# Mixture-of-experts products on TensorE: matmuls of one width issued together, half a weight tile at a time

## The chip, the cores and the metric

One core of a Trainium2 chip runs the whole step as a single launch. The metric is the device time of that launch in microseconds (us), the median of repeated runs on one chip. The kernel is written engine by engine: TensorE (PE), VectorE (DVE), ScalarE (ACT), GpSimd (POOL) and SyncE (SP) each have their own instruction stream, and they wait for each other on semaphores that the program names. All data are fp32.

## What is computed

The program is one inference step of a two-layer backbone over 384 tokens (128 context, 256 latent) of width 1024. Each layer has a mixer (gated linear attention with windowed attention in layer 0, RWKV-7 in layer 1) and then a mixture of experts. Only the mixture of experts bears on this change:

```python
def hier_moe(h, w_grp, b_grp, w_exp, b_exp, w_gate, w_up, w_down):
    ...
    gates = jnp.sum(jax.nn.one_hot(idx, N_EXPERTS, dtype=f32) * wts[..., None], axis=1)
    hid = jax.nn.silu(jnp.einsum('td,edf->tef', t, w_gate)) * jnp.einsum('td,edf->tef', t, w_up)
    hid = hid * gates[..., None].astype(hid.dtype)
    return jnp.einsum('tef,efd->td', hid, w_down).reshape(B, L, D)
```

There are 16 experts (4 groups of 4) a layer; a token goes to two experts of one group. An expert has gate and up matrices of 1024 x 512 each and a down matrix of 512 x 1024.

## The kernel before, in words

**Weights.** All large weights stream from HBM as tiles of 128 partitions x 2048 words (1 MB) through a ring of six slots in SBUF (`ring`). SP (`stream`, L256) issues one DMA a tile, and waits for `w_used` before it overwrites a slot; PE increments `w_used` with the last matmul that reads a tile, and waits in `tile_in` (L277) until a tile has landed. An expert takes exactly six tiles: four of gate/up weights (L1390, `gate_up(e, h, half)`: `h` is the half of the hidden width, `half` the half of the contraction over D = 1024) and two of down weights (L1412, `down(e, f)`, two values of `f` a tile).

**Tokens.** The router sorts (token, expert) pairs by expert; an expert gets at most CAP = 96 rows. If no expert has more, the branch with `gathered_pe`, `gathered_act` and `gathered_dve` runs, as here. `TOKE` holds the expert's 96 tokens, transposed (128 partitions x 8 chunks x 96). In every product the tokens are the stationary operand and the weights move. The 96 tokens are split into MANY = 64 and FEW = 32: the 64 are a stationary block of 64 columns of the array, and two such matmuls (`x` = 0, 1) stand side by side in the two column halves; the 32 are a block of 32 columns, and four such matmuls (`x` = 0 to 3) stand side by side in the four column quarters. So one contraction step `kk` of gate/up is two matmuls of 64 columns x 256 moving columns (L1398) and four of 32 columns x 128 moving columns (L1401), and one step `f` of down is two of 64 x 512 (L1418) and four of 32 x 256 (L1423). The profile records an fp32 matmul as two instructions (two passes over the moving columns), each with its own weight load (PEld).

**One expert on PE** (L1428, `expert`) is, in this order: gate_up(0,0), gate_up(0,1), gate_up(1,0), turn_hidden(0), gate_up(1,1), down 0, turn_hidden(1), down 1, down 2, down 3. In a tile the steps go one after another, and each step issues its 64-wide and then its 32-wide matmuls. `turn_hidden(h)` (L1405) turns the gated hidden rows of half `h` (ACT's silu L1493/L1494, then DVE's product L1577, which signals `s_hid`) with four transposes: a block of 64 rows and one of 32 rows for each of two chunks, in turns. DVE copies the result to `HIDG` (L1580, `s_tts`), the stationary operand of down.

**Around it.** ACT loads the next expert's tokens (L1488), and ACT (L1501) and DVE (L1592) copy an expert's products to `ROWE`, from where ACT's queue sends 96 rows to HBM (L1509). Expert 0 stands ahead of the loop: it takes its tokens straight from a selection matmul, while POOL scatters all token rows to HBM in sorted order (L1618) and reads them back in six blocks (L1622). PE turns these after expert 0 (`turn_sorted`, L1371, L1387), ACT and DVE store them (`TOK`), and expert 1 begins. Experts 1 to 13 are a loop (`pe.Fori`), 14 and 15 stand behind it. In expert 15 three blocks of mixed token rows, gathered back by POOL (L1627) and mixed by DVE (L1559, L1560), are turned between the down products (`turn_mixed`, L1363), and DVE adds them to the state (L1568); then eight banks of last products follow (L1467, L1468).

Of the kernel before, what the change touches and what calls it, by code (L numbers as in the profile page):

```python
# [26 lines left out]
P = 128  # L27
D = 1024
KC = D // P
# [6 lines left out]
HD = 64  # L36
# [7 lines left out]
CAP = 96  # L44
MANY, FEW = 64, 32
# [158 lines left out]
def build(nc, xT, cst, rcst, vec, sinkr, ckT, cv, zgla, zrwkv, wrt, brt, dec2, wa2, wstream,  # L204
# [6 lines left out]
    def sem(name):  # L211
        return ctx.enter_context(nc.semaphore(name))
# [4 lines left out]
    with ctx:  # L217
# [19 lines left out]
        def bank(b, cols=T, at=0):  # L237
            return ps[:, b * 512 + at:b * 512 + at + cols]

        def area(at, words, **dims):  # L240
            v = A[:, at:at + words]
            if not dims:
                return v
            names = " ".join(dims)
            return v.rearrange(f"p ({names}) -> p {names}", **dims)

        w_in = [sem(f"weight_tile_in_slot{i}") for i in range(RING)]
        w_used = sem("weight_tiles_used")
# [28 lines left out]
        def tile_in(pe, n, i=0):  # L277

            pe.wait_ge(w_in[n % RING], i * 16 + 16 * (n // RING + 1))

        def tile(n, **dims):
            names = " ".join(dims)
            return ring[:, n % RING * TILE:(n % RING + 1) * TILE].rearrange(f"p ({names}) -> p {names}", **dims)
# [806 lines left out]
        def moe_block(l, at, end, squares):  # L1090
# [49 lines left out]
            HIDG = area(o4, 4 * CAP, f=4, s=CAP)  # L1140
# [14 lines left out]
            TOKE = area(o7 + 2 * GU, KC * CAP, k=KC, s=CAP)  # L1155
# [194 lines left out]
            with nc.Block() as block:  # L1350
# [8 lines left out]
                def mixed(a, k):  # L1359
                    return bank((2, 6, 2)[a] + k // 4, P, P * (k % 4))  # L1360

                def gathered_pe(pe):
                    def turn_mixed(a):  # L1363
                        pe.wait_ge(s_y, a + 1)
                        if a == 2:
                            pe.wait_ge(s_t0a, 1)
                        for k in range(KC):
                            mm = pe.transpose(mixed(a, k), YR[:, 0, a, P * k:P * k + P], ident)
                        mm.then_inc(s_t0, 1)

                    def turn_sorted():  # L1371
                        pe.wait_ge(s_sell, 1)
                        for y in range(2):
                            for a in range(3):
                                mm = pe.transpose(bank(6 + y, P, P * a)[0:CAP], SELL[:, y, a, :], ident)
                        mm.then_inc(s_turn_l, 1)
                        for g in range(12):
                            b, half = divmod(g, 2)
                            if half == 0:
                                pe.wait_ge(s_rin[b], 16)  # L1380
                            if g == 2:
                                pe.wait_ge(s_gh, 1)
                            if g >= 4:
                                pe.wait_ge((s_hg, s_hd)[half], b - 1)
                            for x in range(4):
                                k = 4 * half + x
                                mm = pe.transpose(bank(TURN_BANKS[g % 4], P, P * x), RB[:, b, P * k:P * k + P], ident)  # L1387
                            mm.then_inc(s_ga, 1)

                    def gate_up(e, h, half):  # L1390
                        tile_in(pe, at + 2 * h + half, e)
                        w = tile(at + 2 * h + half, k=4, w=2, c=256)
                        for kk in range(4):
                            k = 4 * half + kk
                            if (h, half, kk) == (1, 0, 3):
                                pe.wait_ge(s_hid, e * 2 + 1)
                            for x in range(2):
                                pe.matmul(bank(h, 256)[HD * x:HD * x + HD], TOKE[:, k, 0:MANY], w[:, kk, x, :],  # L1398
                                          start=k == 0, stop=k == KC - 1)
                            for x in range(4):  # L1400
                                mm = pe.matmul(bank(2 + h, P)[FEW * x:FEW * x + FEW], TOKE[:, k, MANY:CAP],  # L1401
                                               w[:, kk, x // 2, x % 2 * P:x % 2 * P + P], start=k == 0, stop=k == KC - 1)
                        mm.then_inc(w_used, 1)

                    def turn_hidden(h):  # L1405
                        for c in range(2):
                            pe.transpose(bank(6 + c, MANY), HIDR[HD:P, h, P * c:P * c + P], ident[HD:P, HD:P])
                            r = slice(HD + FEW * c, HD + FEW * c + FEW)
                            mm = pe.transpose(bank(6 + c, FEW, MANY), HIDR[r, h, 256:GU], ident[r, r])  # L1409
                        mm.then_inc(s_tt, 1)  # L1410

                    def down(e, f):  # L1412
                        w = tile(at + 4 + f // 2, f=2, c=D)
                        if f % 2 == 0:
                            pe.wait_ge(s_tts, e * 2 + (f // 2 + 1))
                            tile_in(pe, at + 4 + f // 2, e)
                        for x in range(2):
                            pe.matmul(bank(4, 512)[HD * x:HD * x + HD], HIDG[:, f, 0:MANY], w[:, f % 2, 512 * x:512 * x + 512],  # L1418
                                      start=f == 0, stop=f == 3)
                        if f == 0:  # L1420
                            pe.wait_ge(s_hid, e * 2 + 2)
                        for x in range(4):
                            mm = pe.matmul(bank(5, 256)[FEW * x:FEW * x + FEW], HIDG[:, f, MANY:CAP],  # L1423
                                           w[:, f % 2, 256 * x:256 * x + 256], start=f == 0, stop=f == 3)
                        if f % 2:
                            mm.then_inc(w_used, 1)

                    def expert(e, last=False):  # L1428
                        first = isinstance(e, int) and e == 0
                        if not first:  # L1430
                            pe.wait_ge(s_tok, e)
                        gate_up(e, 0, 0)
                        gate_up(e, 0, 1)
                        gate_up(e, 1, 0)
                        turn_hidden(0)
                        gate_up(e, 1, 1)
                        if not first:
                            pe.wait_ge(s_ous, e)
                            pe.wait_ge(s_ousa, e)
                        down(e, 0)  # L1440
                        turn_hidden(1)
                        down(e, 1)
                        if last:
                            turn_mixed(0)
                        down(e, 2)
                        down(e, 3)
                        if last:
                            turn_mixed(1)
                            turn_mixed(2)

                    pe.wait_ge(s_tf, 2)
                    pe.wait_ge(s_sl, 1)
                    expert(0)
                    turn_sorted()
                    with pe.Fori(1, NE - KEPT) as e:
                        expert(e)
                    expert(NE - 2)
                    expert(NE - 1, last=True)
                    pe.wait_ge(s_gh, 1)
                    pe.wait_ge(s_ous, NE)  # L1460
                    pe.wait_ge(s_ousa, NE)
                    for n, b in enumerate(FINAL_BANKS):
                        if b == 6:
                            pe.wait_ge(s_t0a, 2)
                        if b == 2:
                            pe.wait_ge(s_t0a, 3)
                        pe.matmul(bank(b), ROWE[0:CAP, 0, P * n:P * n + P], GH[0:CAP, 0, :], start=True, stop=False)  # L1467
                        pe.matmul(bank(b), ROWE[0:CAP, 1, P * n:P * n + P], GH[0:CAP, 1, :], start=False,  # L1468
                                  stop=True).then_inc(s_fin, 1)
# [1192 lines left out]
```

## Time and profile before

| | before |
|---|---|
| median of 3 runs | 1827.23 us (1827.18 to 1830.56) |
| the profiled execution's own time | 1828.28 us |
| its span, first to last instruction | 1826.4 us |
| mean granted TensorE clock | 0.957 of full |
| PE busy | 1645.4 us, 90% of the span |
| DVE, ACT, POOL busy | 613.3, 526.5, 265.1 us (34%, 29%, 15%) |
| moved by DMA | 328.33 MB, mean 180 GB/s |

The two mixtures of experts lie at about 383 to 770 us and 1414 to 1800 us of the span. A PE that is shown busy is not a PE at its peak, since the ends of pipelined matmuls are modelled; how long work takes is therefore read here from the starts of neighbouring rows, not from busy sums.

### The profile page before, as it was taken

The numbers are of one execution on the slowest core, as the hardware profiler recorded it, in microseconds if no ns is written. First come the engines' busy times: TensorE is split into PE (matmuls) and PEld (weight loads), VectorE is DVE, ScalarE is ACT, GpSimd is POOL, SyncE is SP. The second block draws the span as 40 slices with busy tenths as digits, with TensorE's granted clock in tenths as the row PEclk, the third lists the DMA queues.
The fourth block names the chain that finished last, engine by engine and source line by source line (L and its number), as shares of the span: only waits on it lengthen the run. The fifth ranks groups of instructions, "written<-read, shape, count | busy, mean of one in ns | idle before, by whom it ended". The sixth has DMA issues, their size and how long they took to land. (4 is left out here: it accounts for less than half of the span.)

```text
span 1826.4 us, 41121 instructions
## 1 busy us (share of the span) xinstructions
PE 1645.4 (90%) x17678; PEld 888.8 (49%) x17678; DVE 613.3 (34%) x1520; ACT 526.5 (29%) x1202; POOL 265.1 (15%) x260
## 2 busy tenths in 40 slices
PE   3997968889999999959998889989877999999997
PEld 1554554453333333435557777777744433333333
DVE  2004762341111111450306766666615111111115
ACT  3114543221111111120135666565413111111112
POOL 0000040020000000010044555555001000000010
PEclk9998998999999999979999999898989999999999
DMA  9225549376878887812200000000033787788891
GB/s 390 98 98 193 226 191 374 119 286 227 287 282 288 289 292 283 313 46 92 104 12 5 6 6 5 5 6 4 6 140 134 282 287 287 285 286 288 286 342 41
DMA packets 54036, 328.33 MB, mean 180 GB/s; under 512 B 6646, under 2 KB 10038, under 8 KB 18712
## 3 DMA queue, kind: packets, MB, share of 16 engines
q1 hardware_dynamic: 43632, 290.07, 43.2%
q0 software_dynamic: 5184, 18.88, 2.6%
q10 hardware_dynamic: 5096, 17.58, 2.5%
q8 instruction: 96, 1.57, 0.4%
q14 instruction: 28, 0.23, 0.0%
HBM read 304.35 MB, written 22.16 MB: 179 GB/s over the span
## 5 line engine op out<-in xcount | busy, mean ns | idle before, releaser
L1398 PE MATMUL ps<-ring,arena 128*64 128x256 f32 x2048 | 336.2, 407 | 6.3 <-ACT arena L1488 5.2
L1401 PE MATMUL ps<-ring,arena 128*32 128x128 f32 x4096 | 219.2, 286 | 0.0
L298 PE MATMUL ps<-HT,ring 128*128 128x384 f32 x544 | 180.6, 496 | 14.2 <-PEq L367 8.2
L1401 PEld LDWEIGHTS ps<-ring,arena 128*32 128x32 f32 x4096 | 81.0, 108 | 198.5 <-issue 198.5
L1577 DVE TENSOR_TENSOR arena<-arena,ps 64x256 f32<-64x256 f32 (+1 forms) x128 | 40.6, 357 | 344.7 <-ACT arena L1494 344.7
L1398 PEld LDWEIGHTS ps<-ring,arena 128*64 128x64 f32 x2048 | 101.9, 135 | 109.7 <-issue 106.9
L1493 ACT ACTIVATE arena<-ps 64x256 f32<-64x256 f32 x64 | 24.1, 377 | 443.1 <-PE ps L1401 443.1
L298 PEld LDWEIGHTS ps<-HT,ring 128*128 128x128 f32 x544 | 105.4, 194 | 89.2 <-issue 19.7
L1418 PE MATMUL ps<-ring,arena 128*64 128x512 f32 x512 | 138.1, 618 | 0.0
L1627 POOL DMA_INDIRECT arena<-moe_rows,arena x12 | 11.4, 952 | 674.1 <-DMA moe_rows<-arena 671.1
L1501 ACT ACTIVATE arena<-ps 32x256 f32<-32x256 f32 x128 | 48.0, 375 | 198.0 <-PE ps L1423 196.9
L298 PE MATMUL ps<-arena,ring 128*128 128x384 f32 x256 | 85.4, 498 | 18.8 <-DVEq L2026 18.8
L1423 PE MATMUL ps<-ring,arena 128*32 128x256 f32 x1024 | 81.8, 391 | 10.1 <-DVE arena L1577 10.1
L1592 DVE COPY arena<-ps 64x512 f32<-64x512 f32 x64 | 44.0, 688 | 135.4 <-PE ps L1423 134.7
L322 PE MATMUL ps<-ring,arena 128*32 128x256 f32 x768 | 55.3, 442 | 23.8 <-DMA ring<-wstream 14.6
L1423 PEld LDWEIGHTS ps<-ring,arena 128*32 128x32 f32 x1024 | 20.1, 108 | 116.2 <-issue 77.9
L298 PEld LDWEIGHTS ps<-arena,ring 128*128 128x128 f32 x256 | 49.8, 195 | 54.5 <-DVEq L2026 19.5
L1580 DVE COPY arena<-ps 128x192 f32<-128x192 f32 x64 | 22.9, 358 | 152.2 <-PE ps L1409 152.2
L2431 PE MATMUL ps<-ring 64*64 64x32 f32 x1536 | 59.3, 228 | 13.0 <-DVE ring L2288 8.3
L2431 PEld LDWEIGHTS ps<-ring 64*64 64x64 f32 x1536 | 53.0, 143 | 36.3 <-DVE ring L2288 17.6
L2431 PE MATMUL ps<-ring,arena 64*64 64x32 f32 x1536 | 61.7, 232 | 2.3 <-DVE arena L2313 2.3
L2431 PEld LDWEIGHTS ps<-ring,arena 64*64 64x64 f32 x1536 | 55.4, 149 | 7.3 <-issue 4.3
(357 smaller groups left out, 2300.6 us busy)
## 6 DMA issues: line engine op xcount, KB each, us to landing
ring<-wstream SPq DMA_DIRECT2D x272, 1024.0 KB, 5.2
moe_rows<-arena ACTq DMA_DIRECT2D x28, 384.0 KB, 4.7
arena<-moe_tokens POOLq DMA_DIRECT2D x12, 512.0 KB, 10.6
moe_rows<-arena ACTq DMA_DIRECT2D x4, 512.0 KB
consts<-cst ACTq DMA_DIRECT2D x1, 1655.0 KB, 17.1
XT<-xT ACTq DMA_DIRECT2D x1, 1536.0 KB, 11.1
yT<-HT SPq DMA_DIRECT2D x3, 384.0 KB, 3.2
arena<-wa SPq DMA_DIRECT2D x1, 1024.0 KB, 4.8
```

The source lines that it names most:

```text
L298: mm = pe.matmul(bank(m % 8), w[:, k, m % 2 * P:m % 2 * P + P], rhs[:, k, :], start=k == 0, stop=k == KC - 1)
L322: mm = pe.matmul(bank(b, 256)[32 * g:32 * g + 32], SC[:, k, :], w[:, a, g, :], start=k == 0, stop=k == KC - 1)
L1398: pe.matmul(bank(h, 256)[HD * x:HD * x + HD], TOKE[:, k, 0:MANY], w[:, kk, x, :], start=k == 0, stop=k == KC - 1)
L1401: mm = pe.matmul(bank(2 + h, P)[FEW * x:FEW * x + FEW], TOKE[:, k, MANY:CAP], w[:, kk, x // 2, x % 2 * P:x % 2 * P + P], start=k == 0, sto ...
L1418: pe.matmul(bank(4, 512)[HD * x:HD * x + HD], HIDG[:, f, 0:MANY], w[:, f % 2, 512 * x:512 * x + 512], start=f == 0, stop=f == 3)
L1423: mm = pe.matmul(bank(5, 256)[FEW * x:FEW * x + FEW], HIDG[:, f, MANY:CAP], w[:, f % 2, 256 * x:256 * x + 256], start=f == 0, stop=f == 3)
L1493: act.activation(HIDR[HD:P, h, 0:256], bank(h, 256)[0:HD], ACT.Silu)
L1501: last = act.activation(ROWE[MANY:CAP, kept, 256 * x:256 * x + 256], bank(5, 256)[FEW * x:FEW * x + FEW], ACT.Copy)
L1577: hid = dve.tensor_tensor(x, x, bank(b, GU - 256 if b > 1 else 256)[HD:P], ALU.mult)
L1580: dve.tensor_copy(HIDG[:, 2 * h:2 * h + 2, :], ps[:, 3072:4096].rearrange("p (f s) -> p f s", f=2)[:, :, 0:CAP]).then_inc(s_tts, 1)
L1592: copy = dve.tensor_copy(ROWE[0:MANY, kept, 512 * x:512 * x + 512], bank(4, 512)[HD * x:HD * x + HD])
L2431: mm = pe.matmul(bank(o, 32, 32 * n)[h], dn(left)[h, d, n], right[h, d, n], start=True, stop=True)
```

## The change

In `gate_up` the four steps of a tile are split by width: `many()` issues the 64-wide matmuls of all four steps, `few()` the 32-wide ones. A tile with `half` = 0 issues `many()` then `few()`, one with `half` = 1 the reverse, so that at a border between two tiles the same width goes on. `turn_hidden` issues its two transposes of 64 rows first and its two of 32 rows then. `down(e, f)` becomes `down_many` and `down_few`, called from `expert` in an order that goes on with the same width from one step to the next. The wait for the second half's hidden product (`s_hid`, e * 2 + 2) moves from between the 64-wide and the 32-wide matmuls of step 0 to behind both. The number and the shapes of matmuls are the same, and so is the code of the other engines.

```diff
+                        def many():
+                            for kk in range(4):
+                                k = 4 * half + kk
+                                for x in range(2):
+                                    mm = pe.matmul(bank(h, 256)[HD * x:HD * x + HD], TOKE[:, k, 0:MANY], w[:, kk, x, :],
+                                                   start=k == 0, stop=k == KC - 1)
+                            return mm
...
+                        if half:
+                            few()
+                            mm = many()
+                        else:
+                            many()
+                            mm = few()
                         mm.then_inc(w_used, 1)
...
                         for c in range(2):
                             pe.transpose(bank(6 + c, MANY), HIDR[HD:P, h, P * c:P * c + P], ident[HD:P, HD:P])
+                        for c in range(2):
                             r = slice(HD + FEW * c, HD + FEW * c + FEW)
                             mm = pe.transpose(bank(6 + c, FEW, MANY), HIDR[r, h, 256:GU], ident[r, r])
                         mm.then_inc(s_tt, 1)
...
-                        down(e, 0)
+                        pe.wait_ge(s_tts, e * 2 + 1)
+                        w = down_tile(e, 0)
+                        down_many(w, 0)
+                        down_few(w, 0)
+                        pe.wait_ge(s_hid, e * 2 + 2)
+                        down_few(w, 1)
                         turn_hidden(1)
-                        down(e, 1)
+                        down_many(w, 1).then_inc(w_used, 1)
                         if last:
                             turn_mixed(0)
-                        down(e, 2)
-                        down(e, 3)
+                        w = down_tile(e, 1)
+                        pe.wait_ge(s_tts, e * 2 + 2)
+                        down_many(w, 2)
+                        down_few(w, 2)
+                        down_few(w, 3)
+                        down_many(w, 3).then_inc(w_used, 1)
```

PE in the loop over experts, before: the last steps of gate_up(1,0), the first turn of hidden rows and the first step of gate_up(1,1). A row is a line of the kernel, what is written and read (`ps` is PSUM, `ring` the weights, `arena` the tokens or hidden rows), the shape of the product and a count of matmuls.

```order
L1398 MATMUL ps<-ring,arena 64x256 x2
L1401 MATMUL ps<-ring,arena 32x128 x4
L1396 ISA
L1398 MATMUL ps<-ring,arena 64x256 x2
L1401 MATMUL ps<-ring,arena 32x128 x4
L1407 MATMUL ps<-consts,arena 128x64
L1409 MATMUL ps<-consts,arena 128x32
L1407 MATMUL ps<-consts,arena 128x64
L1409 MATMUL ps<-consts,arena 128x32
L1398 MATMUL ps<-ring,arena 64x256 x2
L1401 MATMUL ps<-ring,arena 32x128 x4
```

The same place now, from gate_up(0,0) to the end of gate_up(1,1):

```order
L1398 MATMUL ps<-ring,arena 64x256 x8
L1408 MATMUL ps<-ring,arena 32x128 x32
L1398 MATMUL ps<-ring,arena 64x256 x16
L1408 MATMUL ps<-ring,arena 32x128 x12
L1406 ISA
L1408 MATMUL ps<-ring,arena 32x128 x4
L1422 MATMUL ps<-consts,arena 128x64 x2
L1425 MATMUL ps<-consts,arena 128x32 x2
L1408 MATMUL ps<-ring,arena 32x128 x16
L1398 MATMUL ps<-ring,arena 64x256 x8
```

Sixteen pairs of a 64-wide and a 32-wide row became five rows of one width each and a part of a sixth, and the wait of the first turn (ISA) still stands ahead of the last step's 32-wide matmuls of gate_up(1,0).

PE in the same loop, before: down steps 0 and 1 with the second turn between them (steps 2 and 3 repeat the last two rows).

```order
L1418 MATMUL ps<-ring,arena 64x512 x2
L1421 REGISTER_ALU
L1423 MATMUL ps<-ring,arena 32x256 x4
L1407 MATMUL ps<-consts,arena 128x64
L1409 MATMUL ps<-consts,arena 128x32
L1407 MATMUL ps<-consts,arena 128x64
L1409 MATMUL ps<-consts,arena 128x32
L1418 MATMUL ps<-ring,arena 64x512 x2
L1423 MATMUL ps<-ring,arena 32x256 x4
```

The same place now, all four down steps:

```order
L1434 MATMUL ps<-ring,arena 64x512 x2
L1440 MATMUL ps<-ring,arena 32x256 x4
L1460 REGISTER_ALU
L1440 MATMUL ps<-ring,arena 32x256 x4
L1422 MATMUL ps<-consts,arena 128x64 x2
L1425 MATMUL ps<-consts,arena 128x32 x2
L1434 MATMUL ps<-ring,arena 64x512 x4
L1440 MATMUL ps<-ring,arena 32x256 x8
L1434 MATMUL ps<-ring,arena 64x512 x2
```

The 32-wide matmuls of step 1 now stand ahead of the turn, the 64-wide ones of steps 1 and 2 follow each other, and the last 64-wide row runs into the next expert's first one. REGISTER_ALU works out the value for the wait on `s_hid`, which stands there.

## Rows read from the trace of the kernel before

**Rows 1.** Windows, layer 0's loop: PE, PEld, DVE, ACT, POOL (x), clock, DMA share, GB/s.

```profile
440.00:500.00 60.00, 59.37 (x666) 21.68 (x664) 9.08 (x21) 8.88 (x24) 0.00 (x0) 1.00 0.83 297
```

**Rows 2.** Waits, 440 to 740 us: who waited for whom, total us, times, longest.

```profile
ACT arena L1493 <- PE ps L1401: 177.1, 26, 7.7
PE ps L1423 <- DVE arena L1577: 4.1, 13, 0.3
```

**Rows 3.** PE timeline, one expert: start, us, line, out<-in, stationary, moving, count.

```profile
560.68 0.65 PE L1398 MATMUL ps<-ring,arena 128*64 128x256 f32 x4
561.26 0.42 PE L1401 MATMUL ps<-ring,arena 128*32 128x128 f32 x8
561.62 0.65 PE L1398 MATMUL ps<-ring,arena 128*64 128x256 f32 x4
...
568.19 0.27 PE L1407 MATMUL ps<-consts,arena 64*128 64x64 f32 x1
...
568.94 0.65 PE L1398 MATMUL ps<-ring,arena 128*64 128x256 f32 x4
...
572.70 1.08 PE L1418 MATMUL ps<-ring,arena 128*64 128x512 f32 x4
574.10 0.64 PE L1423 MATMUL ps<-ring,arena 128*32 128x256 f32 x8 [0.32 <-DVE arena L1577]
...
577.00 1.08 PE L1418 MATMUL ps<-ring,arena 128*64 128x512 f32 x4
578.01 0.64 PE L1423 MATMUL ps<-ring,arena 128*32 128x256 f32 x8
578.58 1.08 PE L1418 MATMUL ps<-ring,arena 128*64 128x512 f32 x4
...
591.42 0.27 PE L1407 MATMUL ps<-consts,arena 64*128 64x64 f32 x1
```

**Rows 4.** PE timeline, stages before the experts: runs of one width.

```profile
281.58 3.66 PE L322 MATMUL ps<-ring,arena 128*32 128x256 f32 x64
291.47 1.07 PE L322 MATMUL ps<-ring,arena 128*32 128x256 f32 x16 [1.41 <-DMA ring<-wstream]
...
212.17 0.87 PE L655 MATMUL ps<-arena 128*64 128x128 f32 x6
```

**Rows 5.** Windows: layer 1's mixer, with many small matmuls (columns as rows 1).

```profile
1311.80:1314.80 3.00, 3.00 (x113) 2.37 (x113) 1.66 (x6) 2.88 (x7) 0.00 (x0) 1.00 0.03 5
```

**Rows 6.** Windows: a stretch in which the weight stream is never idle (columns as rows 1).

```profile
280.00:290.00 10.00, 9.41 (x129) 6.36 (x128) 1.71 (x6) 1.70 (x5) 0.00 (x0) 1.00 1.01 424
```

**Rows 7.** PE timeline, layer 0: start of expert 0, its end, start of expert 1.

```profile
382.58 0.65 PE L1398 MATMUL ps<-ring,arena 128*64 128x256 f32 x4 [0.58 <-ACT arena L1255]
...
405.81 0.86 PE L1375 MATMUL ps<-consts,arena 128*96 128x128 f32 x6
...
416.08 0.65 PE L1398 MATMUL ps<-ring,arena 128*64 128x256 f32 x4 [2.45 <-ACT arena L1488]
...
417.10 1.12 PE L1398 MATMUL ps<-ring,arena 128*64 128x256 f32 x4
418.15 0.66 PE L1401 MATMUL ps<-ring,arena 128*32 128x128 f32 x8
```

**Rows 8.** POOL's reads of the sorted token rows, six a layer (line L1622).

```profile
L1622 POOL DMA_DIRECT2D arena<-moe_tokens x12: 527/550/580, 388.0 to 1422.5; - x12
DMA to landing us min/median/max: 4.0/10.6/18.4
```

**Rows 9.** DVE timeline, expert 15 of layer 0: second turn's copy, product copies.

```profile
761.39 0.36 DVE L1580 COPY arena<-ps 128x192 f32<-128x192 f32 x1 [1.48 <-PE ps L1409]
...
768.06 1.39 DVE L1592 COPY arena<-ps 64x512 f32<-64x512 f32 x2
```

**Rows 10.** PE timeline, same place: start of the eight last products.

```profile
769.55 0.88 PE L1467 MATMUL ps<-arena 96*128 96x384 f32 x2 [0.37 <-issue]
```

**Rows 11.** POOL's gathers of rows to mix, six a layer (line L1627).

```profile
L1627 POOL DMA_INDIRECT arena<-moe_rows,arena x12: 933/937/1007, 727.1 to 1764.5; - x12
DMA to landing us min/median/max: 11.0/15.3/18.9
```

More of the change, by code:

```diff
@@ L1392, in gate_up, with few @@
                         w = tile(at + 2 * h + half, k=4, w=2, c=256)
[L1393 to L1402, printed above, removed]
+                        def many():
[5 more added lines that the diff above has]
+                            return mm
+                        def few():
+                            for kk in range(4):
+                                k = 4 * half + kk
+                                if (h, half, kk) == (1, 0, 3):
+                                    pe.wait_ge(s_hid, e * 2 + 1)
+                                for x in range(4):
+                                    mm = pe.matmul(bank(2 + h, P)[FEW * x:FEW * x + FEW], TOKE[:, k, MANY:CAP],
+                                                   w[:, kk, x // 2, x % 2 * P:x % 2 * P + P], start=k == 0, stop=k == KC - 1)
+                            return mm
+                        if half:
[4 more added lines that the diff above has]
+                            mm = few()
                         mm.then_inc(w_used, 1)
@@ L1410, in turn_hidden, with down_tile, down_many, down_few @@
                         mm.then_inc(s_tt, 1)
[L1412 to L1416, printed above, removed]
+                    def down_tile(e, j):
+                        tile_in(pe, at + 4 + j, e)
+                        return tile(at + 4 + j, f=2, c=D)
+                    def down_many(w, f):
                         for x in range(2):
[L1418 to L1421, printed above, removed]
+                            mm = pe.matmul(bank(4, 512)[HD * x:HD * x + HD], HIDG[:, f, 0:MANY],
+                                           w[:, f % 2, 512 * x:512 * x + 512], start=f == 0, stop=f == 3)
+                        return mm
+                    def down_few(w, f):
                         for x in range(4):
@@ L1424, in down @@
                                            w[:, f % 2, 256 * x:256 * x + 256], start=f == 0, stop=f == 3)
-                        if f % 2:
-                            mm.then_inc(w_used, 1)
+                        return mm
                     def expert(e, last=False):
```

## The prediction

> **What bounds the kernel now.** I read the windows first. In the loop over experts PE is busy 59.37 of 60 us at the full granted clock, VectorE and ScalarE 9 us each, and the DMA engines 0.83 of the time [rows 1]. The waits say the same: ScalarE waits for PE (177 us in 300), PE for others only 4.1 us, 0.3 a time, always in the same place: the product of the second hidden half [rows 2]. So an expert lasts as long as PE takes for it: 591.42 - 568.19 = 23.23 us from one first turn to the next [rows 3].
>
> Is PE at its peak in there? The timeline of one expert gives the steps from start to start [rows 3]: a gate/up step is 0.58 us of 64-wide and 0.36 us of 32-wide matmuls, a down step 1.01 and 0.57 us, a turn 0.75 us, and the first down step 1.40 us for its 64-wide part because of the wait. These add up: 16 x 0.94 + 4 x 1.58 + 2 x 0.75 + 0.39 = 23.2 us.
>
> Then I looked for a place where matmuls of one width follow each other without a change. Before the experts, 32-wide matmuls with 256 moving columns, four side by side, do so with new weights each: 64 instructions (16 passes of four) in 3.66 us, 16 instructions (4 passes) in 1.07 us [rows 4]. Twelve more passes cost 2.59 us, 0.216 us a pass of 256 columns, that is 0.108 for 128 and 0.43 for 512. The 64-wide kind shows the same pace: six in a row with 128 columns last 0.87 us; less the 0.27 that one takes at the end, that is 0.60 us for five steps with a start of some 0.05, 0.11 each [rows 4]. With these paces the steps of [rows 3] split:
>
> - gate/up 64-wide: 0.58 = 2 passes x 0.216 + 0.15; 32-wide: 0.36 = 2 x 0.108 + 0.14.
> - down 64-wide: 1.01 = 2 x 0.43 + 0.15; 32-wide: 0.57 = 2 x 0.216 + 0.14.
>
> So each change of width costs 0.14 to 0.15 us, whatever the columns: the array is filled and emptied without overlap. An expert pays this some 40 times, and that is a quarter of its time.
>
> **What the change does, part by part.**
>
> *Gate/up and down.* The columns stay: 32 passes x 0.216 + 32 x 0.108 + 8 x 0.43 + 8 x 0.216 = 15.5 us an expert. The runs of one width become, around the loop: four 64-wide ones (down 3 with the next expert's gate_up(0,0); gate_up(0,1) with (1,0); gate_up(1,1) with down 0; down 1 with 2) and five 32-wide ones ((0,0) with (0,1); (1,0); (1,1); down 0 with 1; down 2 with 3). That is 4 x 0.15 + 5 x 0.14 = 1.3 us where 20 x 0.29 = 5.8 us were paid.
>
> *Turns.* Four transposes in 0.75 us had a change at each; two of these go. Bounds: 0.38 us, if each pair costs as much as one, and 0.75. I take 0.75 - 2 x 0.14, about 0.5, so 1.0 an expert for 1.5.
>
> *The moved wait.* PE needs the second hidden product 1.40 us after down's first matmul starts [rows 3]. It now has down 0 of both widths ahead of it: 0.86 + 0.15 + 0.43 = 1.44 us. Gate_up(1,1) now ends with its 64-wide matmuls, so ScalarE may start slightly later. I leave 0.1 us for 0.39. Queued behind this wait are down 1 and the turn; DVE, which copies the turn, waits for them, and then down 2 for DVE, with 1 us of 64-wide matmuls (down 1) as cover against a copy of 0.36 us [rows 9].
>
> Sum for an expert: 15.5 + 1.3 + 1.0 + 0.1 = 17.9 us, **5.3 us less**. Bounds from the turns, the wait and the rounding: 17.5 to 18.4.
>
> *Weights.* Six tiles of 1.05 MB and 0.39 MB of rows an expert are 6.68 MB. Where the stream is never idle it moves 424 GB/s [rows 6], so 15.8 us: the stream hides below 17.9 us, but with a tenth to spare instead of a third. It is the next in line.
>
> *Expert 0.* It begins at 382.58 and ends at 405.81 [rows 7]; it will end near 400.5. But expert 1 needs the six blocks of sorted rows, and the last one lands 18.4 us after an issue at about 390.7 (the first issue is at 388.0, each takes about 0.55 us) [rows 8]: at 409.1. From there, 0.9 us of transposes, the last copies and the load of tokens remain, some 3.8 us: expert 1 starts at about 412.9 instead of 416.08 [rows 7]. Gain 3.2 of the 5.3 us; the rest turns into a wait for POOL's reads. They share the engines with a weight stream that comes sooner, so 1 us either way.
>
> *Expert 15.* Behind the second turn, DVE is the bound: from its copy at 761.39 to the end of the products' copies at 769.45 it has no pause to speak of [rows 9], and the last products start right then, at 769.55 [rows 10]. What PE gains behind that turn (3 x 1.58 us become 3.9) is lost: 0.8 us. Gain 4.5 us.
>
> *All.* A layer: 3.2 + 14 x 5.3 + 4.5 = 82 us; two layers 164 us. Against the profiled execution's 1828.3 us (1.1 above the median of the runs, so the same within a thousandth) that is 1664. I add 2 us: the gathers of rows to mix take up to 18.9 us to land [rows 11], and will come nearer to their use in expert 15. Forecast: **1666 us**.
>
> **A rule that speaks against it.** The rows above show weight loads that hide: 0.216 us a pass in the run of 64 is the same 0.84 ns a column as the step from 256 to 512 moving columns within the experts (1.08 - 0.65 = 0.43 us for 512 columns in two passes) [rows 3, 4], so nothing of a load is in it. The Trainium skill, "TensorE: Matmul & The Clock Gate", section "The mechanism" of Part 3, says that a weight load overlaps running matmuls only if its row group differs; here all products use all 128 rows. By that rule every pass would pay its load, and the change would lose most of its gain; the trace does not agree for the 32-wide kind.
>
> **Rivals.**
>
> 1. *The weight stream becomes the bound.* For: 0.83 of the engines' time is taken at 23.23 us an expert [rows 1], which is 19.3 us of busy time, more than 17.9. Against: that includes the waiting of each transfer's first packets, which a denser stream would hide, and in [rows 6] it moves 424 GB/s. If 19.0 us an expert stay, the gain is 14 x 4.2 + 3.2 + 3.4 = 65 us a layer: 1697. Chance 0.15.
> 2. *PE cannot be fed.* In long 32-wide runs of gate/up one matmul must start every 0.108 / 4 = 27 ns. For: the longest run in [rows 4] has only one in 54 ns. If that were the limit, 32 passes would cost 0.108 more, 3.5 us an expert: a gain of 1.8 us, about 1771 at worst; halfway, 1717. Against: 113 instructions in 3.00 us, one in 26.5 ns, in the mixer [rows 5]. Chance 0.07.
> 3. *Loads are paid in every pass.* The first pass in a run is longer than the next by some 0.05 us (64-wide) and 0.03 us (32-wide) for its load; paid 40 times each, that is 3.2 us an expert, a gain of 2.1 us: some 1760. That is the page's rule as a mechanism of this kernel. Chance 0.03.
> 4. *The change does only half of what it says:* the pause stands between steps of 64-wide matmuls too (the trace shows their runs only with 128 columns on one column half [rows 4]). 20 x 0.15 = 3.0 instead of 0.6 us, a gain of 2.9 us: 1738. Chance 0.04.
> 5. *Slower:* PE loses its full clock. In expert 1, after PE has stood idle 2.45 us, a 64-wide step takes 418.15 - 417.10 = 1.05 us instead of 0.58, as at half the clock [rows 7]. If PE now stops for each tile, the same could go on through the loop; an expert at half clock would take about 15.5 x 2 + 2.4 = 33.4 us, 15.5 more than at full. It would outweigh the gain of 5.3 us from a third of the experts on, and give some 2110 us in all. Against: 1.00 in the loop now, with waits of 0.3 us in it [rows 1, 2]. Chance 0.02.
>
> **How the numbers follow.** The forecast has 0.68 and lies between 1652 (turns at 0.38 us, restart 1 us sooner, rounding) and 1682 (18.4 us an expert). Rival 1 adds 1682 to 1706, and with it the low end of rival 2: 0.84 in all. So the range is 1652 to 1706. Remaining chances lie above it. About 0.2% can be told from no change: faster by more 0.97, the same 0.01, slower 0.02.
>
> **What would show it.** In the profile after: experts 17.9 us apart by the first turn; 64-wide runs of gate/up of 16 passes at 0.216, 32-wide ones at 0.108 us; the wait in front of down 1's 32-wide matmuls at or below 0.2 us; DMA share near 0.95 and no PE wait for `ring`; expert 1 near 413 us, released by the row blocks. PE waits for weight tiles, or passes longer than these, would show where I am wrong.

## The result, and the profile after

The changed kernel takes 1682.41 us (median of 4 runs, 1680.07 to 1689.40), the kernel before beside it 1827.20: a ratio of 0.921, interval 0.918 to 0.924. Five more runs (experiment 10) give 1684.39 us and the same ratio. The forecast was 1666, the range 1652 to 1706. So the direction and most of the size came as worked out, and 16 us are missing. The profiled execution takes 1680.41 us with a span of 1678.6; that is 147.8 less than the span before, and this difference is what the rows below split up.

The head of the page after: span, then busy time, share of the span and instructions of each engine.

```profile
span 1678.6 us, 41121 instructions
PE 1494.4 (89%) x17678; PEld 957.6 (57%) x17678; DVE 613.7 (37%) x1520; ACT 526.4 (31%) x1202; POOL 265.2 (16%) x260
```

PE does the same products in 151 us less busy time, and DVE and ACT are busy as long as before. The same stretch of the loop as [rows 1], in the windows of the changed kernel (us, PE, PEld, DVE, ACT, POOL with counts, clock, DMA share, GB/s):

```profile
440.00:500.00 60.00, 60.00 (x854) 34.96 (x852) 11.80 (x28) 12.31 (x33) 0.00 (x0) 1.00 0.97 369
```

The clock stays at 1.00, PE gets through 854 instructions in place of 666, and the DMA share goes from 0.83 to 0.97. Read alone, that share says that the weight stream is all but the bound. The waits of the changed kernel from 420 to 660 us (who for whom, total, times, longest), which answer to [rows 2], say otherwise:

```profile
ACT arena L1518 <- PE ps L1398: 129.7, 27, 7.5
PEld ps L1440 <- DVE arena L1602: 4.7, 13, 0.4
```

These are two lines of the list; no wait of PE for `ring` stands in it. ACT still waits for PE, and the wait for the second hidden product is now one of the weight load alone (0.4 us at most). The PE timeline of one expert after, which answers to [rows 3] (start, us, line, out<-in, stationary, moving, count):

```profile
573.00 0.34 PE L1422 MATMUL ps<-consts,arena 64*128 64x64 f32 x2
573.26 0.25 PE L1425 MATMUL ps<-consts,arena 32*128 32x32 f32 x2
573.44 1.08 PE L1408 MATMUL ps<-ring,arena 128*32 128x128 f32 x32
574.45 1.95 PE L1398 MATMUL ps<-ring,arena 128*64 128x256 f32 x16
576.23 1.03 PE L1434 MATMUL ps<-ring,arena 128*64 128x512 f32 x4
577.19 1.16 PE L1440 MATMUL ps<-ring,arena 128*32 128x256 f32 x16
578.28 0.33 PE L1422 MATMUL ps<-consts,arena 64*128 64x64 f32 x2
...
584.32 1.96 PE L1408 MATMUL ps<-ring,arena 128*32 128x128 f32 x64
586.21 3.67 PE L1398 MATMUL ps<-ring,arena 128*64 128x256 f32 x32
589.81 1.08 PE L1408 MATMUL ps<-ring,arena 128*32 128x128 f32 x32
590.82 0.33 PE L1422 MATMUL ps<-consts,arena 64*128 64x64 f32 x2
```

From first turn to first turn it is now 590.82 - 573.00 = **17.82 us**, where 17.9 was forecast and 23.23 was before. Sixty-four 32-wide instructions (16 passes) last 586.21 - 584.32 = 1.89 us: 16 x 0.108 = 1.73 and one change of 0.16. Thirty-two 64-wide ones (16 passes) last 3.60 us: 16 x 0.216 = 3.46 and one change of 0.14. A turn is 0.44 us, where about 0.5 was taken.

So the loop gives what was promised. The missing microseconds lie at its two ends. This is the PE timeline between expert 0 and expert 1 of layer 0 after, which answers to [rows 7]; a bracket holds the idle time ahead and what ended it:

```profile
384.47 1.95 PE L1398 MATMUL ps<-ring,arena 128*64 128x256 f32 x16 [0.58 <-ACT arena L1255]
...
402.44 0.86 PE L1375 MATMUL ps<-consts,arena 128*96 128x128 f32 x6
...
407.71 1.82 PE L1387 MATMUL ps<-consts,arena 128*128 128x128 f32 x8 [0.97 <-DMA arena<-moe_tokens]
412.38 5.58 PE L1387 MATMUL ps<-consts,arena 128*128 128x128 f32 x24 [2.84 <-DMA arena<-moe_tokens]
420.41 2.59 PE L1398 MATMUL ps<-ring,arena 128*64 128x256 f32 x16 [2.45 <-ACT arena L1513]
```

Expert 0 ends 18.0 us after its start (23.2 before), but expert 1 starts 35.9 us after that same start, where it was 33.5 before. PE waits for the sorted row blocks. Two windows of that stretch, one during the waits and one behind them (columns as above):

```profile
408.00:412.00 4.00, 1.53 (x8) 1.13 (x6) 0.69 (x1) 0.60 (x1) 0.00 (x0) 0.50 1.02 422
412.40:418.00 5.60, 5.56 (x24) 4.68 (x24) 1.38 (x2) 1.80 (x3) 0.00 (x0) 0.50 0.33 134
```

While PE waits, the DMA engines move 422 GB/s, about as much as in [rows 6]; of the 1.69 MB in this window, 0.88 MB are weights that nobody needs yet, and 0.44 MB belong to the blocks. Then the ring is full and the engines rest. In and after its waits PE is granted 0.50 of its clock (1.2 GHz), and it has not the whole clock back when expert 1 begins: 16 64-wide instructions take 2.59 us here and 1.95 in expert 0. POOL's reads of these blocks after, to be held against [rows 8]:

```profile
L1647 POOL DMA_DIRECT2D arena<-moe_tokens x12: 527/551/580, 392.2 to 1352.4; - x12
DMA to landing us min/median/max: 5.9/15.2/21.2
```

The median landing went from 10.6 to 15.2 us. The last block of layer 0 now lands at 415.95 us, 31.5 us after expert 0 began, where it was 26.5 us. The six reads are issued within 2.7 us and land one after another: in layer 0 before, the last four at 398.19, 401.96, 405.30 and 409.06 us, and now at 407.67, 412.33, 414.21 and 415.95. At the other end, expert 15 of layer 0 (PE timeline after, the place of [rows 9, 10]):

```profile
695.94 1.94 PE L1368 MATMUL ps<-consts,arena 128*128 128x128 f32 x8 [4.15 <-DVEq L1596]
697.68 1.48 PE L1492 MATMUL ps<-arena 96*128 96x384 f32 x2
```

PE stands idle for 4.15 us before the last mixed block, and the last products begin at a granted clock of 0.50 (1.48 us for a pair that took 0.88 before [rows 10]). DVE's mixing (DVE timeline) waits for the gathers just ahead of it:

```profile
691.60 0.75 DVE L1584 TENSOR_SCALAR arena<-arena 128x1024 f32<-128x1024 f32 x1 [3.37 <-DMA arena<-moe_rows,arena]
```

POOL's gathers after, which answer to [rows 11]:

```profile
L1652 POOL DMA_INDIRECT arena<-moe_rows,arena x12: 933/937/1007, 663.4 to 1629.7; - x12
DMA to landing us min/median/max: 8.1/13.6/21.9
```

By stage, before against after, taken from the two timelines (layer 0, layer 1; "first turn" is DVE's copy behind it). The forecast's terms are divided at the first turns here: of expert 1's 5.3 us of gain, 2.9 lie ahead of its first turn, so that 3.2 becomes 6.1 for the first stage and 4.5 becomes 1.6 for the last.

| stage | forecast, a layer | measured, layer 0 | measured, layer 1 |
|---|---|---|---|
| start of expert 0 to expert 1's first turn | -6.1 | -0.6 | -0.5 |
| the next 14 first turns | -74.2 | -75.7 | -75.7 |
| expert 15's first turn to the end of its last products (layer 1: to their start) | -1.6, and +2 for both layers together | +4.4 | -1.2 |

That sums to -149.3 us; the other stages, which the change doesn't touch, gave 1.5 back (1.9 of them ahead of the first expert).

### The profile page after: what moved, and what is told of

It reads as the page before. It is cut to its first block and busy times, and to the rows that moved or that the text cites. A ratio compares the mean times of both kernels' runs of the same rounds, so it can differ in the third digit from the quotient of the medians.

```text
span 1678.6 us, 41121 instructions
## 1 busy us (share of the span) xinstructions
PE 1494.4 (89%) x17678; PEld 957.6 (57%) x17678; DVE 613.7 (37%) x1520; ACT 526.4 (31%) x1202; POOL 265.2 (16%) x260
## 5 line engine op out<-in xcount | busy, mean ns | idle before, releaser
L1398 PE MATMUL ps<-ring,arena 128*64 128x256 f32 x2048 | 243.2, 385 | 6.3 <-ACT arena L1513 5.2
L1398 PEld LDWEIGHTS ps<-ring,arena 128*64 128x64 f32 x2048 | 141.9, 137 | 97.0 <-issue 36.0
L1408 PE MATMUL ps<-ring,arena 128*32 128x128 f32 x4096 | 133.8, 278 | 0.0
L1434 PE MATMUL ps<-ring,arena 128*64 128x512 f32 x512 | 129.8, 605 | 0.0
L1408 PEld LDWEIGHTS ps<-ring,arena 128*32 128x32 f32 x4096 | 107.7, 111 | 27.0 <-issue 25.4
L322 PE MATMUL ps<-ring,arena 128*32 128x256 f32 x768 | 55.9, 445 | 25.1 <-DMA ring<-wstream 15.8
L1440 PE MATMUL ps<-ring,arena 128*32 128x256 f32 x1024 | 71.2, 388 | 0.0
L1440 PEld LDWEIGHTS ps<-ring,arena 128*32 128x32 f32 x1024 | 23.4, 108 | 68.9 <-issue 51.9
## 6 DMA issues: line engine op xcount, KB each, us to landing
arena<-moe_tokens POOLq DMA_DIRECT2D x12, 512.0 KB, 15.2
```

What stands on the lines that cost most here:

```text
L322: mm = pe.matmul(bank(b, 256)[32 * g:32 * g + 32], SC[:, k, :], w[:, a, g, :], start=k == 0, stop=k == KC - 1)
L1398: mm = pe.matmul(bank(h, 256)[HD * x:HD * x + HD], TOKE[:, k, 0:MANY], w[:, kk, x, :], start=k == 0, stop=k == KC - 1)
L1434: mm = pe.matmul(bank(4, 512)[HD * x:HD * x + HD], HIDG[:, f, 0:MANY], w[:, f % 2, 512 * x:512 * x + 512], start=f == 0, stop=f == 3)
```

## The experiments

Experiments 1 to 4 and 8 are one execution each, and their readings rest on the timelines more than on the times.

**1. The turns alone.** The kernel before, with the transposes of 64 rows ahead of those of 32:

```diff
                         for c in range(2):
                             pe.transpose(... 64 rows ...)
+                        for c in range(2):
                             pe.transpose(... 32 rows ...)
```

> Before, with the transposes of hidden rows issued by height alone. Theory (each change of shape on the array costs about 0.145 us): two of the five changes of a turn go, and the changed kernel's trace shows 0.44 us for a turn instead of 0.75, so an expert takes 23.23 - 0.62 = 22.6 us and the kernel about 1827 - 28 x 0.62 = 1809 us. Rival (the gain of the turns is hidden behind the wait for the second hidden product): 0.31 us an expert or less, 22.9 us, 1818 us.

Measured: 1810.98 us beside 1826.73. The PE timeline of the loop:

```profile
540.86 0.33 PE L1407 MATMUL ps<-consts,arena 64*128 64x64 f32 x2
541.12 0.25 PE L1410 MATMUL ps<-consts,arena 32*128 32x32 f32 x2
541.30 0.65 PE L1398 MATMUL ps<-ring,arena 128*64 128x256 f32 x4
...
563.47 0.33 PE L1407 MATMUL ps<-consts,arena 64*128 64x64 f32 x2
```

A turn is 0.44 us for 0.75, and an expert 22.61 for 23.23: 0.31 a turn for two changes fewer, 0.155 each. A change of the height of transposes costs what a change of width does.

**2. Gate/up alone.** The kernel before with the new `gate_up` (`many()`, `few()`, the reverse in every second tile), and turns and down as before. The diff is that part of the change.

> Before, with only gate/up grouped by width (tiles with half 1 in reverse); turns and down as before. Theory (a constant price a change of width): 27 of the changes go, 27 x 0.145 = 3.9 us, against which the wait for the second hidden product grows by some 0.1 us since the last 64-wide matmuls now stand right before down: 19.4 us an expert, kernel about 1725 us. Rival (the price belongs to other things, such as a new bank or a new accumulation step): an expert stays within 1 us of 23.2.

Measured: 1731.27 us beside 1826.73, so this part gives most of the gain. The PE timeline of the loop:

```profile
543.05 0.27 PE L1422 MATMUL ps<-consts,arena 64*128 64x64 f32 x1
...
556.00 1.95 PE L1408 MATMUL ps<-ring,arena 128*32 128x128 f32 x64
557.88 3.67 PE L1398 MATMUL ps<-ring,arena 128*64 128x256 f32 x32
...
562.50 0.27 PE L1422 MATMUL ps<-consts,arena 64*128 64x64 f32 x1
```

An expert takes 19.45 us, 3.78 less than before, for 27 changes fewer with 0.13 us of longer wait for the hidden product set against them: 0.145 a change. Sixty-four instructions in 1.88 us are one per 29 ns, so PE is fed (rival 2), and a pass doesn't pay its load (rival 3).

**3. Without the reversal.** The changed kernel, each gate/up tile as `many()` and then `few()`:

```diff
-                        if half:
-                            few()
-                            mm = many()
-                        else:
-                            many()
-                            mm = few()
+                        many()
+                        mm = few()
```

> The changed kernel without the reversal: every gate/up tile issues its 64-wide, then its 32-wide matmuls. Theory: twelve runs of one width an expert instead of nine, 3 x 0.145 = 0.43 us more: 18.2 to 18.3 us an expert, and the kernel some 28 x 0.43 = 12 us slower than the changed one, about 1693 us. Rival (the weight stream, busy 0.98 of the time, is what sets 17.82 us): no change at 17.8 us.

Measured: 1686.66 us. The PE timeline has 573.52 - 555.35 = 18.17 us from first turn to first turn:

```profile
555.35 0.33 PE L1418 MATMUL ps<-consts,arena 64*128 64x64 f32 x2
...
559.69 1.07 PE L1436 MATMUL ps<-ring,arena 128*32 128x256 f32 x16
560.69 0.33 PE L1418 MATMUL ps<-consts,arena 64*128 64x64 f32 x2
...
573.52 0.33 PE L1418 MATMUL ps<-consts,arena 64*128 64x64 f32 x2
```

The expert is longer by 0.35 us as soon as PE has more changes to pay. That is less than the 0.43 of three changes, because the wait at down 0 went: its 16 32-wide instructions take 560.69 - 559.69 = 1.00 us here and 1.09 in the changed kernel. With that, three changes cost 0.44 us. Had the weight stream set the 17.82 us, these would have been hidden: PE sets them.

**4. One width, the old order.** The kernel before, whose four 32-wide products of a gate/up step are replaced by two 64-wide ones with 128 moving columns:

```diff
-                            for x in range(4):
-                                mm = pe.matmul(bank(2 + h, P)[FEW * x:FEW * x + FEW], TOKE[:, k, MANY:CAP],
-                                               w[:, kk, x // 2, x % 2 * P:x % 2 * P + P], start=k == 0, stop=k == KC - 1)
+                            for x in range(2):
+                                mm = pe.matmul(bank(2 + h, P)[HD * x:HD * x + HD], TOKE[:, k, FEW:CAP],
+                                               w[:, kk, x, 0:P], start=k == 0, stop=k == KC - 1)
```

> Before, in its old order, with the 32-wide gate/up products replaced by 64-wide ones of 128 moving columns, two side by side (they take other tokens and leave half of the weights' columns out; the passes and columns in time stay the same). Theory (the width change is what costs): no pause is left in a gate/up step, 2 x 0.216 + 2 x 0.108 = 0.65 us instead of 0.94; 31 changes go, so 23.23 - 4.5 = 18.7 us an expert, though nothing is grouped. Rival (the pause comes with a change of bank, of moving length or of accumulation step, whatever the width): 0.94 us a step and 23.2 us an expert stay.

Measured: 1707.65 us; an expert takes 559.80 - 540.91 = 18.89 us. Two steps in the PE timeline:

```profile
540.91 0.27 PE L1407 MATMUL ps<-consts,arena 64*128 64x64 f32 x1
...
542.36 0.60 PE L1398 MATMUL ps<-ring,arena 128*64 128x256 f32 x4
542.79 0.39 PE L1401 MATMUL ps<-ring,arena 128*64 128x128 f32 x4
543.01 0.60 PE L1398 MATMUL ps<-ring,arena 128*64 128x256 f32 x4
...
559.80 0.27 PE L1407 MATMUL ps<-consts,arena 64*128 64x64 f32 x1
```

A step is 543.01 - 542.36 = 0.65 us, three passes of 0.216 and no pause at all, though the two products still alternate between different moving sizes, banks and weights. So what costs 0.14 to 0.15 us is the change of the stationary block's width itself, neither the order nor the new accumulator. A step also has two products fewer here, but four side by side cost no pause by themselves: experiment 2 has sixteen such passes in a row without one. The Trainium skill, "TensorEngine Tiling (Array Packing)", "Key Properties", says that a change of the tiling mode, as against a change of the tile, drains TensorE. The trace agrees as far as a pause at each such change shows, with 0.58 + 0.36 us a step before [rows 3] and 0.65 here.

**5. The weight stream held for the row blocks.** The changed kernel; SP waits in each layer for the sixth block (in the branch without sorted blocks POOL signals the same semaphore itself) before it issues the tiles of expert 1:

```diff
                     route_sp(sp)
+                    sp.wait_ge(s_rin[5], 16)
                     stream(sp, end)
...
                 def general_pool(pool):
+                    pool.sem_inc(s_rin[5], 16)
```

> The changed kernel, with SP holding the refills of the weight ring in each mixture until the sixth block of sorted rows has landed. Theory (the gap between expert 0 and expert 1 is long because the refills, asked for sooner, share the DMA engines with the scatter and the six blocks): the sixth block lands near 16 us after the start of expert 0 instead of 31, expert 1 then starts about 10.3 us after the end of expert 0 as it did before (ScalarE and VectorE storing the blocks bound it), 7 us sooner in each layer: about 1667 us. Rival (the blocks are slow by themselves): expert 1 starts where it did, 36 us after expert 0. Second rival (the held tiles come too late): experts 1 and 2 wait for the ring, and the gain is lost, about 1680 us.

Measured: **1662.23 us** (1661.36 to 1663.01), a ratio of 0.9086 to before, interval 0.9069 to 0.9104, beside 0.921 for the changed kernel. The reads of the blocks, and PE between expert 0 and 1:

```profile
L1648 POOL DMA_DIRECT2D arena<-moe_tokens x12: 527/554/580, 391.7 to 1343.1; - x12
DMA to landing us min/median/max: 3.6/7.5/9.5
```

```profile
384.62 1.95 PE L1399 MATMUL ps<-ring,arena 128*64 128x256 f32 x16 [0.58 <-ACT arena L1255]
...
405.83 4.56 PE L1388 MATMUL ps<-consts,arena 128*128 128x128 f32 x40 [1.50 <-ACT arena L1504]
412.83 1.95 PE L1399 MATMUL ps<-ring,arena 128*64 128x256 f32 x16 [2.45 <-ACT arena L1514]
```

The slowest block lands after 9.5 us instead of 21.2, PE no longer waits for any, and in layer 0 expert 1 starts 28.2 us after expert 0 instead of 35.9. Its first 16 instructions take 1.95 us, so the stretch at half the clock is gone too. Up to expert 1's first turn that makes 9.4 us in each layer, 7.7 and 6.6 of them by the earlier start. The stream catches up: no wait for `ring` follows in the loop, which stays at 17.82 us an expert.

**6. The prefetch held for the gathers.** The changed kernel; SP issues the mixture's own tiles, and waits for the last gathered rows before it prefetches for the stage behind:

```diff
                     route_sp(sp)
+                    stream(sp, at + N_MOE)
+                    sp.wait_ge(s_yin[2], 32 * l + 32)
                     stream(sp, end)
```

> The changed kernel, with SP holding the six tiles of the next block until POOL's gathers of rows to mix have landed. Theory (layer 0's last turn of mixed rows waits 4.15 us because the gathers share the engines with the prefetch, while layer 1, which has none, does not wait): the last gather lands some 16 us after its issue instead of 21.9, the wait goes, and the last products keep the full clock (0.88 us a pair instead of 1.48): 4 to 6 us less, about 1675 us. Rival (the gathers are slowed by the last experts' own tiles): the wait stays, within 1 us of 1680.

Measured: 1682.95 us (1676.45 to 1685.20), no less than the changed kernel. In its place the edit works. The PE timeline of expert 15's end in layer 0, and what follows it:

```profile
691.79 1.06 PE L1370 MATMUL ps<-consts,arena 128*128 128x128 f32 x8 [0.69 <-DVEq L1598]
693.22 0.88 PE L1494 MATMUL ps<-arena 96*128 96x384 f32 x2 [0.37 <-issue]
...
704.72 5.44 PE L1757 MATMUL ps<-arena,consts 128*128 128x384 f32 x16 [0.91 <-ACT arena L1764]
```

The idle time ahead of the last block falls from 4.15 to 0.69 us, and the products start at full speed; the slowest gather lands after 15.3 us instead of 21.9, and the idle 3.37 us of DVE ahead of the mixing are gone. From the first turn's copy (679.78 here, 680.49 in the changed kernel) to the next stage (704.72 and 709.90) it is 24.9 us instead of 29.4: 4.5 us, of which the next stage takes up to 0.9 as a wait of its own. The profiled executions differ by 4 us, the medians don't. The medians leave the worth of this edit open.

**7 and 9. Both holds.** Both edits together, twice, on two chips.

> Both holds together. Theory: the two gains lie in different places and add, 14 + 5 us: about 1662 us. Rival (what is saved at the head returns as waits for weights in the loop): not below 1670 us.

> Both holds once more, with more runs and beside the changed kernel on the same chip. Theory (14 to 18 us from the hold at the head, 5 from the one at the tail, both shown by the traces): 20 us below the changed kernel, 1655 to 1665 us, where the spread comes from the granted clock in layer 1's mixer, which no version touches. Rival (the tail's hold is worth nothing, as the median of that hold alone would have it): the same as the hold for the blocks alone, 1662 us.

Measured: 1658.96 us (1655.49 to 1664.68), then 1663.91 (1656.68 to 1666.56): ratios 0.906 and 0.909 to the kernel before, intervals 0.9035 to 0.9086 and 0.9065 to 0.9112. Against the hold for the blocks alone (0.9086) no difference is shown by the times. The stage itself is shorter: from the copy behind expert 15's first turn to the end of the last products, layer 0 takes 24.0 us in both profiled executions and 29.2 in experiment 5. A likely reason for the scatter stands in a stage that none of these edits touches, the mixer of layer 1. Windows from 870 to 1260 us (columns as above), experiment 5, then the second run of both holds:

```profile
870.00:1260.00 390.00, 340.96 (x6786) 280.12 (x6784) 250.62 (x591) 221.39 (x497) 183.66 (x159) 0.93 0.02 5
```

```profile
870.00:1260.00 390.00, 342.14 (x6722) 282.38 (x6720) 250.28 (x586) 215.57 (x487) 180.88 (x158) 0.90 0.02 5
```

The granted clock is 0.93 and 0.90, and from the first to the last of the stage's most frequent products (L2458 and L2460) it is 351.5 and 359.9 us. The difference of 8.4 us is more than the edit at the tail is worth; experiment 6 has a clock of 0.94 here, experiment 7 one of 0.90. The mean clock of whole executions points the same way: with both holds, the three that took 1655.5 to 1656.7 us had 0.952 to 0.955, the six that took 1662.1 to 1666.6 us had 0.943 to 0.949. Why the clock of this stage differs stays open.

**8. Half the steps.** The changed kernel, with two of the four contraction steps in each gate/up tile, so that PE has less to do for the same stream:

```diff
-                            for kk in range(4):
+                            for kk in (2, 3):
...
```

The same stands in both `many()` and `few()`, and the first of the two steps left starts the sum.

> The changed kernel with half of the gate/up steps left out (each tile's first two), so that PE needs 17.82 - 16 x 0.216 - 16 x 0.108 = 12.6 us an expert while the weights to load stay the same. It measures where the weight stream becomes the bound. Theory (the stream at its pace of 424 GB/s): 6.68 MB take 15.8 us, an expert lasts 15.8 to 16.5 us and PE waits for the ring. Rival (a busy share of 0.98 at 376 GB/s means that the stream is already at its limit in the changed kernel): 17.5 to 17.8 us an expert.

Measured: 1614.92 us. An expert takes 15.8 us; the windows, and the waits from 440 to 600 us:

```profile
440.00:500.00 60.00, 50.54 (x600) 23.48 (x596) 12.81 (x30) 12.60 (x34) 0.00 (x0) 1.00 1.01 424
```

```profile
PEld ps L1434 <- DMA ring<-wstream: 20.9, 11, 2.2
PE ps L1434 <- DMA ring<-wstream: 16.0, 10, 1.7
```

This is what a loop bound by the stream looks like: PE 50.5 of 60 us, waits for `ring`, 424 GB/s at a share of 1.01. The floor of 15.8 us is the forecast's 6.68 MB at the rate of [rows 6], and 2 us below the changed kernel's expert. A share of 0.97 at 369 GB/s was not that bound.

**10. The changed kernel again**, beside experiment 9 on the same chip, unedited.

> The changed kernel, unaltered, for comparison on the same chip as the version with both holds: 1680 to 1690 us, as measured before.

Measured: 1684.39 us (1679.09 to 1690.48), ratio 0.921, interval 0.9185 to 0.9235. Experiment 9 beside it, with both holds, is 20 us faster.

## Why the prediction was right, and where it was off

**The price of a change of width: right.** 0.14 to 0.15 us was forecast; experiments 1 to 4 measure 0.14 to 0.155, and 4 shows that the width is the cause.

**Long runs at 0.216 and 0.108 us a pass: right**, up to 16 passes. That settles rivals 2, 3 and 4. Rival 3 was the rule of the Trainium skill, "TensorE: Matmul & The Clock Gate", "The mechanism", that a weight load overlaps running matmuls only where row groups differ. By it a pass would be longer; all products here have the same 128 rows and fresh weights in each pass, and 16 passes stay at 1.89 us. The trace does not agree with this sentence taken alone. The same section also lets a load go ahead into a background weight buffer, which the prediction left out; with that the trace agrees as far as the loads hide.

**The expert: 17.82 us for 17.9.** The turn was the term off, 0.44 us for 0.5, twice; the wait was left at 0.1 us and is a wait of the weight load. Fourteen periods gave 75.7 us a layer, 1.5 more than forecast.

**The weight stream: right, and too much feared.** Rival 1 took the 0.83 share of [rows 1] for 19.3 us of need. Experiment 8 puts the need at 15.8 us, as the prediction's sum from [rows 6] did, and experiment 3 shows PE setting the period.

**The failed step: the restart of expert 1.** "They share the engines with a weight stream that comes sooner, so 1 us either way" was the sentence. It named the mechanism and gave it far too small a price. The last block was forecast at 409.1 us, where it landed before, and came at 415.95. Of these 6.9 us, 1.9 are a later start of expert 0; 2.3 are a later issue (7.7 us after expert 0's start, where it was 5.4; experiment 5, with the stream held, has 7.1, so 1.7 of them have another cause, which stays open); and 2.7 are a longer landing. The transposes at a granted clock of 0.50 add 0.7. So of 6.1 us of gain up to expert 1's first turn 0.6 came, and the two layers lack 11 us. But the landing is not bound by the reads themselves: with the stream held the last takes 9.5 us. So it was not only a gain that didn't come, it was 9.4 us a layer that lay open, more than the forecast had for the whole head. [Rows 8] could have warned, if read as a queue: the 4.0 to 18.4 us are six reads that land one after another, beside the stream 3.3 to 3.8 us apart from the third on, and with the stream held 1.2 to 1.3 us apart in layer 1 of experiment 5. The 18.4 us were a share of the engines, and were carried over as if they belonged to the transfer.

**The tail of layer 0: mis-sized.** For late gathers 2 us were allowed in all. They took up to 21.9 us to land instead of 18.9 (15.3 with the prefetch of the next stage held, experiment 6), and with expert 15 shorter the mixing met them: a gain of 1.6 us became a loss of 4.4 (4.15 us of idle PE, and last products that are 1.8 us longer for a start at half the clock). In layer 1 the gain was 1.2, and in layer 0 too as soon as the prefetch was held (24.0 us for 25.2), 0.4 less than forecast.

The account: the heads lack 11.1 us, the tails 4.4, the untouched stages 1.5, and the loops gave 3.0 more. These 14.0 us, with half a microsecond of rounding in the forecast, are what lies between the gain of 162.3 us forecast against the profiled execution before (1828.28) and the 147.9 measured (1680.41). **Rival 5** (half the clock) was wrong for the loop, 1.00 in its windows, but its mechanism showed at both ends, behind waits of PE. Not every wait brings it: in experiment 5 the 2.45 us of idle time ahead of expert 1 are the same, and its first instructions run at full speed.

## What to carry to other kernels

Count the changes of the stationary block's size in an inner loop, and price them from the trace by comparing a run of one size with the alternation; putting equal sizes together, across borders of tiles too, changes neither the number nor the shapes of the products. When a loop gets faster, look at each transfer beside its stream that someone waits for at the loop's ends: the stream fills in sooner, the transfer lands later, and holding the stream until it has landed can be free where the stream has time to spare. Here an expert takes 17.82 us and its weights need 15.8, and after the hold no wait for `ring` followed. Take the share of busy DMA engines for an upper bound of what a stream needs, and bytes over the rate of a stretch that is never idle for the need itself.

## What was not expected of the hardware

- Six reads of 512 KB, alone on the engines, land within 9.5 us, and beside the weight stream within 21.2. The Trainium skill, "DMA: Bandwidth & Descriptors", "Queues, rings and completion order", says that an engine takes the packets of its queues in turn; the trace agrees as far as both transfers get slower together: the weight tiles issued from 392 to 417 us land after 11.1 us, with a median of 7.4 over the whole execution.
- The DMA share is no measure of need: 0.83 at 297 GB/s [rows 1], 0.97 at 369 and 1.01 at 424 for the same kind of stream.
- A change of height between transposes of 64 and 32 rows costs 0.155 us (one execution, experiment 1), like a change of width.
